# Loading the half-unit weight tiles of the second gate in another order, in a two-layer decoder trunk on one core

## What is computed

```python
def mixer_layer(x, ...):
    xn = rmsnorm(x, ln_g)
    proj = xn @ w_in
    q, k, v, z_a, x_b, z_b, g_a, g_b = jnp.split(proj, SPLIT_IDX, axis=-1)
    ...
    merged = jax.nn.sigmoid(g_a) * (o_a @ w_a) + jax.nn.sigmoid(g_b) * (o_b @ w_b)
    return x + merged @ w_o, S_new, conv_new, h_last
```

## Time and profile before

| | |
|---|---|
| median of 3 runs | 1902.68 us (1901.27 to 1905.5) |
| profiled execution, its own time | 1901.83 us |
| its span, first to last instruction | 1900.0 us |
| TensorE's granted clock, of full speed | 0.997 |
| PE busy | 1880.8 us (99%) |
| DVE busy | 1262.8 us (66%) |
| ACT busy | 807.3 us (42%) |
| second gate in block form, layer 0 | 780.9 to 827.6 us of the span |
| second gate in block form, layer 1 | 1715.1 to 1761.2 us |

### The profile page before, as it was taken

How to read it: one execution, slowest core, us unless ns; L and a number is a source line. 1 busy time by engine, 2 the same in 40 slices (tenths; PEclk the granted TensorE clock), 3 DMA queues, 4 the chain that set the end, 5 groups by cost and what they waited for, 6 DMA issues and landing times.

```text
span 1900.0 us, 32236 instructions
## 1 busy us (share of the span) xinstructions
PE 1880.8 (99%) x12984; PEld 1762.9 (93%) x12984; DVE 1262.8 (66%) x2144; ACT 807.3 (42%) x1293; POOL 284.6 (15%) x399
## 2 busy tenths in 40 slices
PE   8999999999999999999999999999999999999998
PEld 7899898898899999999998988988989999999997
DVE  8775665665766877864487656657557678878445
ACT  5432332423427776542344324234124377766223
POOL 2221120120231200100022201202102422001000
PEclk9999999999999999999999999999999999999999
DMA  6435544453443333543354445534544533327332
GB/s 219 129 125 166 160 149 128 164 178 110 149 150 93 107 104 97 154 124 120 99 174 158 147 124 172 178 110 149 169 126 137 165 102 111 95 83 193 103 123 78
DMA packets 114786, 257.48 MB, mean 136 GB/s; under 512 B 11822, under 2 KB 52254, under 8 KB 114510
## 3 DMA queue, kind: packets, MB, share of 16 engines
q1 hardware_dynamic: 84350, 156.00, 26.4%
q0 software_dynamic: 30144, 99.41, 16.5%
q10 hardware_dynamic: 144, 0.00, 0.0%
HBM read 196.55 MB, written 49.12 MB: 129 GB/s over the span
## 4 chain that ended last, share of the span: by engine, by line
PE 87%; DVE 5%; ACT 3%; DMA 2%; DVEq 1%; issue 1%; ACTq 1%; SPq 0%
PE bank L1944 20%; PE bank L1946 20%; PE bank L1945 20%; PE bank L2014 4%; PE bank L2015 4%; PE bank L2016 4%; PE last L2032 2%; DMA w_raw<-in_w_units 1%; PE last L2014 1%; PE last L2015 1%; PE last L2016 1%; PE bank L2282 1%; PE bank L2285 1%; PE bank L2284 1%; PE sums L2147 1%
## 5 line engine op out<-in xcount | busy, mean ns | idle before, releaser
L1944 PE MATMUL bank<-xn_hi,w_hi 128*128 128x296 f32 (+1 forms) x2176 | 650.8, 299 | 0.4 <-DVE w_lo L531 0.3
L1946 PE MATMUL bank<-xn_lo,w_hi 128*128 128x296 f32 (+1 forms) x2176 | 646.4, 297 | 0.0
L1945 PE MATMUL bank<-xn_hi,w_lo 128*128 128x296 f32 (+1 forms) x2176 | 645.7, 297 | 0.0
L1944 PEld LDWEIGHTS bank<-xn_hi,w_hi 128*128 128x128 f32 x2176 | 409.2, 188 | 7.0 <-issue 4.3
L1945 PEld LDWEIGHTS bank<-xn_hi,w_lo 128*128 128x128 f32 x2176 | 409.6, 188 | 1.0
L1946 PEld LDWEIGHTS bank<-xn_lo,w_hi 128*128 128x128 f32 x2176 | 408.8, 188 | 0.0
L524 ACT ACTIVATE w_hi<-w_raw 128x1024 fp32r<-128x1024 f32 x229 | 241.0, 1056 | 347.0 <-DMA w_raw<-in_w_units 344.5
L531 DVE TENSOR_TENSOR w_lo<-w_raw,w_hi 128x1024 fp32r<-128x1024 f32 x229 | 280.7, 1229 | 88.9 <-ACT w_hi L524 82.1
L1944 PE MATMUL bank<-oa_hi,w_hi 128*128 128x296 f32 (+1 forms) x512 | 153.7, 300 | 0.0
L1945 PE MATMUL bank<-oa_hi,w_lo 128*128 128x296 f32 (+1 forms) x512 | 151.9, 297 | 0.0
L1946 PE MATMUL bank<-oa_lo,w_hi 128*128 128x296 f32 (+1 forms) x512 | 151.7, 296 | 0.0
(11 more groups left out here) (331 smaller groups left out, 3543.6 us busy)
## 6 DMA issues: line engine op xcount, KB each, us to landing
w_raw<-in_w_units SPq DMA_DIRECT2D x199, 512.0 KB, 3.6
S<-in_state_ret POOLq DMA_DIRECT2D x64, 512.0 KB, 4.8
out_ret_s<-S POOLq DMA_DIRECT2D x64, 512.0 KB, 6.2
w_raw<-in_w_units SPq DMA_DIRECT2D x122, 256.0 KB, 3.2
vst<-v_scr SPq DMA_DIRECT2D x8, 512.0 KB, 4.1
out_ret_p<-Sp POOLq DMA_DIRECT2D x8, 512.0 KB, 5.7
w_raw<-in_w_units POOLq DMA_DIRECT2D x16, 256.0 KB, 4.7
v_scr<-vtok_hi SPq DMA_DIRECT2D x16, 160.0 KB
```

The source lines that it names most:

```text
L1944: pe.matmul(ps, w_hi[:, slot, cols], x_hi, start=first, stop=False)
L1945: pe.matmul(ps, w_lo[:, slot, cols], x_hi, start=False, stop=False)
L1946: return pe.matmul(ps, w_hi[:, slot, cols], x_lo, start=False, stop=last)
```

## The change

The parts of a pair are loaded in the order A11, S1, S2, S3, S4, A12, A22 instead of A11, S1, S2, A12, S3, S4, A22. The ring slot of a part follows its place in the new order. The products stay in their order, and so do the lists of ACT, DVE, POOL and PE. The load at place p waits for the product whose part stood at place p - 8, which shifts three waits:

| load of pair t+1 | waited for this product of pair t | waits now for |
|---|---|---|
| S3 | A12 | S2 (one product earlier) |
| S4 | S3 | S3 |
| A12 | S2 | S4 (three products later) |
| A22 | S4 | (A12, done long before; issued right behind the load of A12) |

In the first eight, S3 goes out with S2 (it went with S4), and A12 goes out behind S4 (it went with S2). The load of the third unit of the o_b product waits for one product more.

```diff
 PART_FROM = ((0, 0), (1, 0), (0, 0), (0, 1), (1, 0), (0, 1), (1, 1))
+LOAD_ORDER = (A11, S1, S2, S3, S4, A12, A22)
...
+PART_AT = [n // PRODUCTS * PRODUCTS + LOAD_ORDER[n % PRODUCTS] for n in range(PART_UNITS)]
+
+
+def part_place(n):
+
+    return n // PRODUCTS * PRODUCTS + LOAD_ORDER.index(n % PRODUCTS)
+
+
 def part_slot(l, n):
 
-    return (n + RING * l) % PART_RING
+    return (part_place(n) + RING * l) % PART_RING
...
-            return 16 * sum(1 for m in range(l + 1) for k in range(PART_UNITS if m < l else n + 1)
-                            if part_slot(m, k) == part_slot(l, n))
+            return 16 * sum(1 for m in range(l + 1) for k in range(PART_UNITS)
+                            if (m < l or part_place(k) <= part_place(n)) and part_slot(m, k) == part_slot(l, n))
...
-                for n in range(PART_UNITS):
-                    if n < PART_RING:
-                        sp.wait_ge(unit_done, l * UNITS_LAYER + B_AT - RING + n // 2 + 1)
+                for place, n in enumerate(PART_AT):
+                    if place < PART_RING:
+                        sp.wait_ge(unit_done, l * UNITS_LAYER + B_AT - RING + place // 2 + 1)
                     else:
-                        sp.wait_ge(part_done, l * PART_UNITS + n - PART_RING + 1)
+                        sp.wait_ge(part_done, l * PART_UNITS + PART_AT[place - PART_RING] + 1)
...
-                    sp.wait_ge(part_done, l * PART_UNITS + PART_UNITS - 2 * (B_AT + RING - at) + 2)
+                    place = PART_UNITS - 2 * (B_AT + RING - at)
+                    sp.wait_ge(part_done, l * PART_UNITS + max(PART_AT[place:place + 2]) + 1)
```

## The result

| | before | changed |
|---|---|---|
| median, 9 runs each | 1901.98 us (1901.27 to 1905.5) | 1908.60 us (1906.56 to 1910.19) |
| span of the profiled execution | 1900.0 us | 1907.4 us |
| second gate, layer 0: start of the first A11 to start of the last A22 | 44.93 us | 47.90 us |
| the same, layer 1 | 44.48 us | 47.64 us |
| both blocks | 89.41 us | 95.54 us |

What follows compares the result with a forecast made beforehand. PE, busy 99% of the span, was taken to bound the kernel. Block delays less swallowed stalls gave +5.2 us, so 1901.83 became 1907.0, plus 0.85 for the median: 1907.9 us, range 1901.8 to 1912.5.

Steps and rivals of the forecast that it cites:

- +5.2 us forecast for the blocks: Second gate, both layers: S2 delays in pairs 1 to 3, less stalls already ahead of S3, together +5.2 us.
- The gain is bounded by PE's stalls, 2.5 us: Second gate's two blocks: PE loses about 2.5 us in all, 0.13% of the run, so no measurable gain.
- A12's load goes out at A22's moment, and S2 waits over ACT's copy: Pairs 1 to 3, each layer: A12 issued three products later; hidden under 3.0 us to landing (2.9 in layer 1).
- From landing to PE's S2: ACT's way from A12's landing through high part, tanh and copy into snap to PE's S2: 1.68 us.
- L = 4.0: A12's load: issue to landing taken as 4.0 us, between 2.9 and 5.0, with POOL's DMA 1 to 2 us ahead.
- The stalls ahead of S3 are swallowed: PE's existing waits ahead of S3, 0.43, 0.59 and 0.68 us, absorb part of the new S2 delay.
- DVE's path ends within 0.1 of PE's own: Second path, A12's low part to S3: DVE gives S3 at 800.19, PE's own path 800.1.
- The late third unit of o_b is free: Start of o_b: load at 825.98 instead of 824.34 costs nothing; without DVE's cover, 1 us a layer.
- Rival 2: A12's load meets POOL's DMA head on in every pair, landing near 5.0 us: +11.2 us, 1913.9 us; chance 0.12.
- The step from blocks to time: Whole kernel: 1907.0 us from the profiled execution, plus 0.85 for the median of three runs, gives 1907.9 us.
- -1.7 at L = 2.9: Both blocks: if A12 lands in 2.9 us or less, only regained stalls ahead of S3 are left, -1.7 us.
- The formula that the prediction took from the Trainium skill: A12's load: 2.0 us plus bytes over 436e3 per us, 2.6 us for 256 KB; wait hidden, sum -1.7 us.

Runs made afterwards that it cites:

- ACT-first run: Changed kernel, but ACT makes the high part of A12 only after copying A11's bank into snap, pairs 1 to 3: 1906.27 us, ratio 1.0020.

## Why the prediction was right

Forecast 1907.9 us in a range of 1901.8 to 1912.5, measured 1908.6; +5.2 us forecast for the blocks, +6.1 measured. By its steps:

- *The gain is bounded by PE's stalls, 2.5 us.* Right: the best block of all, 87.60 us, is 1.8 under before.
- *A12's load goes out at A22's moment, and S2 waits over ACT's copy.* Right, six times. From landing to PE's S2 I had 1.68 us; it is 1.54 (796.45 to 797.99), since PE starts 0.47 after the copy's start where I had 0.58, and ACT starts on landing. The restart costs 0.10 (the second matmul starts 0.24 behind the first where 0.14 is usual), not 0.07.
- *L = 4.0.* The six landings have a mean of 4.27 us. Every one lies above the 2.9 of the earlier trace rows, for the reason given: POOL's DMA was 1.0 to 2.1 us ahead. This choice carried the forecast; with L at 2.9 the sign would have been wrong. I made it from three landings, none of them of a load 1 to 2 us behind POOL's DMA. One such was in the same trace: S3's load at 787.56, 1.1 us behind POOL's DMA of 786.47, landed in 4.2. What was argued then is shown now by the held-back DMA and by its removal.
- *The stalls ahead of S3 are swallowed.* Right: 1.49 us of the three are gone, 0.16 and 0.12 of others stand in the pairs 1. The sum: 7.0 us ahead of S2, less 1.2 ahead of S3 and 0.1 elsewhere, plus 0.4 of restarts, is the measured 6.1.
- *DVE's path ends within 0.1 of PE's own.* Right in pair 1 of layer 0 (0.12), and the ACT-first run shows it alone.
- *The late third unit of o_b is free.* Right: ACT waited 0.99 us for it, at 833.61, and PE had no wait from 829 on through the next 70 us.
- Rival 2, a meeting head on in every pair with L near 5.0, did not come; single landings were that long (4.8 here, 5.6 in another run).
- *The closeness of the totals is in part luck.* L was 0.27 us too short, worth 1.6 us over six turns, and the way from landing to S2 was 0.14 too long, which took back 0.8. The step from blocks to time added 0.85 us for a median of three runs that stood at 1902.68; with nine runs it is 1901.98, and the distance between the medians is 6.6 us where I had 5.2. The layers were 2.8 and 2.45 forecast and came out at 2.97 and 3.16. My range was also drawn too narrow for what it says: by my own -1.7 at L = 2.9 and 6 us for each us of L, L from 2.9 to 4.9 gives 1901.0 to 1913.3 before any scatter.

The formula that the prediction took from the Trainium skill ("DMA: Bandwidth & Descriptors", "Anatomy of one DMA") is fitted there to DMAs that GpSimd issues, and A12's load is issued by SP, so it was not a formula for this load. Its 2.6 us lies within what A12's load took with nothing beside it, 2.4 to 3.0 us in the kernel without the accumulating DMA for S3. I had also written that the trace disagrees in this stage, from three loads; A12's own loads in the kernel before, ahead of POOL's DMA in all six turns, took 2.4 to 2.9. The formula has no term for a neighbour, and that term, some 1.2 to 2 us, was the whole case.

## What to carry to other kernels

When a load is moved, ask what the move does to the distance between it and the other transfers, not only how much time it has left: here three products of lateness were all but free without a neighbour and cost 5 to 6 us beside an accumulating DMA that the same edit had pulled forward. Look at what is queued behind the instruction that waits for the load; putting one copy ahead of it on ACT and one block of work on DVE took off most of the loss. And a gap that is removed by reordering an engine's list can come back at another product, as in three kernels here, so count all gaps of the stage, not the one aimed at.

## What the runs showed of the hardware

A12's load by SP, 256 KB, took 2.4 to 3.0 us in all six turns when no accumulating DMA was near, 2.6 to 2.8 with one going out 0.6 to 1.5 us behind it (three turns of the kernel with S3's load late), and 3.6 to 5.5 us with one 0.5 to 2.1 us ahead (all turns of the changed kernel, of its repetition but one, and of the one with A22 apart). The distance alone does not settle it: in pair 0 it took 3.0 to 3.8 us with one 1.7 to 1.8 us ahead in three kernels. Nor is such a neighbour the only thing that slows a load: S1's load of pair 3 in layer 0 of the changed kernel went out 4.3 us behind one and took 4.9 us, for a reason that stays open. The accumulating DMA itself took up to 6.8 us in the kernel with S3's load late, against 3.7 to 5.5 before; no experiment was about that.

I had not expected what a long gap does to PE. In the kernel with S3's load late, the copy came 2.6 us late once. PE's row there, then the stretches ahead of it, behind it, and the next one (length; busy us of PE, PEld, DVE, ACT, POOL with their instructions; granted clock of PE; share of the DMA engines; GB/s):

```profile
1747.67 0.40 PE L2295 MATMUL bank<-right,w_hi 128*128 128x288 f32 x1 [2.44 <-ACT snap L1127]
```

```profile
1744.00:1747.60 3.60, 1.23 (x10) 1.00 (x8) 1.86 (x3) 1.32 (x4) 0.00 (x0) 1.00 0.88 284
1747.70:1752.40 4.70, 4.70 (x24) 4.70 (x25) 3.99 (x7) 3.00 (x7) 0.85 (x1) 0.64 0.37 61
1752.50:1754.00 1.50, 1.50 (x14) 1.50 (x13) 1.06 (x2) 1.06 (x3) 0.00 (x0) 1.00 0.25 27
```

The granted clock was full before the gap, 0.64 on the mean of the next 4.7 us, and full again after that; 14 of the 24 matmuls in that stretch, from the ninth behind the gap on, started 0.24 us apart instead of 0.13: the lower of the clock's two levels, 1.2 GHz. It cost some 1.5 us on top of the gap. Two other profiles with a gap of over 2 us (2.08 with A12 one product later, 2.41 with A22 apart) show the same, with a granted clock of 0.66 and 0.64 behind it; none of the blocks with gaps up to the changed kernel's 1.74 does. In these three profiles the stall cost more than itself.
